# Modulation lanes gathered one block later, two multiplications moved behind the last gating, and attention heads weighed, paired and carried two steps deep

## The reference

```python
c_act = jax.nn.silu(c)
for i in range(DEPTH):
    mod = c_act @ mod_w[i] + mod_b[i]
    sh1, sc1, g1, sh2, sc2, g2, sh3, sc3, g3 = jnp.split(mod, 3 * N_SUB, axis=-1)
    h = modulate(rmsnorm(x, norm_g[i, 0]), sh1, sc1)
    x = x + FFN_RES * g1[:, None, :] * swiglu(h, ffn_w13[i, 0], ffn_w2[i, 0])
    h = modulate(rmsnorm(x, norm_g[i, 1]), sh2, sc2)
    ...
    m = mla_mixer(h, positions, mla_w_in[j], ...)
    x = x + g2[:, None, :] * m
    ...
```

## Time and profile before

| | |
|---|---|
| time, median of 3 runs | 1790.68 us (1790.57 to 1794.25) |
| the profiled execution's own time | 1786.12 us |
| its span, first to last instruction | 1784.3 us |
| mean granted clock of TensorE | 0.996 |
| TensorE busy with matmuls | 1700.4 us, 95% of the span |
| VectorE, ScalarE, GpSimd busy | 1289.4, 939.7 and 86.6 us |
| the chain that ended last | PE 62%, DVE 18%, issue 10%, ACT 8% |

### The profile page before, as it was taken

How to read it: one execution, slowest core, us unless ns; L and a number is a source line. 1 busy time by engine, 2 the same in 40 slices (tenths; PEclk the granted TensorE clock), 3 DMA queues, 4 the chain that set the end, 5 groups by cost and what they waited for, 6 DMA issues and landing times.

```text
span 1784.3 us, 32112 instructions
## 1 busy us (share of the span) xinstructions
PE 1700.4 (95%) x11300; PEld 1525.6 (85%) x11300; DVE 1289.4 (72%) x2157; ACT 939.7 (53%) x1667; POOL 86.6 (5%) x151
## 2 busy tenths in 40 slices
PE   6999999999999999999999999999999999999998
PEld 5899989888999889998778888899977788988886
DVE  6888878768888888866556666689687465556665
ACT  1444457644444444445665555545377755555553
POOL 2000011200000000000001000100000000000000
PEclk9999999999999999999999999999899999999999
DMA  9888866757888788864335666354532154446562
GB/s 349 305 299 305 279 180 201 161 212 258 297 305 263 269 301 297 301 182 143 118 95 133 208 186 190 104 179 145 159 95 78 48 186 159 149 133 200 183 185 67
DMA packets 123656, 352.76 MB, mean 198 GB/s; under 512 B 9850, under 2 KB 52874, under 8 KB 114224
## 3 DMA queue, kind: packets, MB, share of 16 engines
q1 hardware_dynamic: 108128, 262.18, 45.7%
q10 hardware_dynamic: 12432, 78.65, 13.8%
q0 software_dynamic: 3008, 10.74, 1.9%
HBM read 347.31 MB, written 4.22 MB: 197 GB/s over the span
## 4 chain that ended last, share of the span: by engine, by line
PE 62%; DVE 18%; issue 10%; ACT 8%; ACTq 1%; DMA 1%; POOL 1%; DVEq 1%; POOLq 0%
PE ps L829 39%; PE ps L1062 8%; DVE arena L358 4%; PE ps L1063 4%; DVE w_lo L195 3%; ACT w_hi L1116 2%; DVE w_lo L1127 2%; ACT w_hi L189 2%; PE ps L2992 1%; PE ps L3078 1%; DMA resid<-in_x 1%; DVE act_s L1195 1%; DVE resid L1319 1%; ACTq L332 1%; DVE arena L2685 1%
## 5 line engine op out<-in xcount | busy, mean ns | idle before, releaser
L829 PE MATMUL ps<-t_both,w_hi 128*128 128x256 f32 x3952 | 730.3, 286 | 12.8 <-DVE t_both L758 5.7
L829 PEld LDWEIGHTS ps<-t_both,w_hi 128*128 128x128 f32 x3952 | 617.7, 191 | 30.8 <-issue 15.6
L829 PE MATMUL ps<-t_both,w_lo 128*128 128x256 f32 x1976 | 560.4, 284 | 1.0 <-issue 1.0
L829 PEld LDWEIGHTS ps<-t_both,w_lo 128*128 128x128 f32 x1976 | 378.5, 192 | 0.2
L195 DVE TENSOR_TENSOR w_lo<-raw,w_hi 128x1024 fp32r<-128x1024 f32 x240 | 289.2, 1224 | 120.1 <-ACT w_hi L189 119.8
L1127 DVE TENSOR_TENSOR w_lo<-raw,w_hi 128x1024 fp32r<-128x1024 f32 x258 | 313.6, 1221 | 80.5 <-ACT w_hi L1116 80.5
L1116 ACT ACTIVATE w_hi<-raw 128x1024 fp32r<-128x1024 f32 x258 | 268.1, 1053 | 111.4 <-PE ps L829 71.6
L189 ACT ACTIVATE w_hi<-raw 128x1024 fp32r<-128x1024 f32 x240 | 248.4, 1053 | 142.5 <-PE ps L829 99.0
L1062 PE MATMUL ps<-t_both,w_hi 128*128 128x512 f32 x640 | 226.7, 398 | 0.0
L829 PE MATMUL ps<-w_hi,g_hi 128*128 128x512 f32 x440 | 174.8, 397 | 8.1 <-DVE g_lo L1198 6.0
L1063 PE MATMUL ps<-t_both,w_lo 128*128 128x256 f32 x640 | 179.7, 281 | 0.0
(11 more groups left out here) (367 smaller groups left out, 1730.2 us busy)
## 6 DMA issues: line engine op xcount, KB each, us to landing
raw<-in_stream SPq DMA_DIRECT2D x498, 512.0 KB, 4.6
arena<-in_mod_w ACTq DMA_DIRECT2D x72, 1024.0 KB, 7.3
grow<-gate_scratch POOLq DMA_DIRECT2D x6, 512.0 KB, 7.2
u_scratch<-u_keep ACTq DMA_DIRECT2D x1, 3072.0 KB, 36.9
arena<-u_scratch POOLq DMA_DIRECT2D x8, 256.0 KB, 3.5
small<-in_small POOLq DMA_DIRECT2D x1, 1368.0 KB, 11.4
resid<-in_x POOLq DMA_DIRECT2D x1, 1024.0 KB, 18.5
arena<-in_mem POOLq DMA_DIRECT2D x1, 1024.0 KB, 5.5
```

What stands on the lines that cost most here:

```text
L829: last = TE.matmul(out, lhs, rhs, start=start and i == 0, stop=stop and i == 2)
```

## The change

- In `pe_body` the gather moves from behind block 0 to behind block 1, and in `act_body` `mod_take` from ahead of the first silu to ahead of the second.
- In the closing body `dve_body` does products 4 and 5 no longer ahead of the second gating, but behind it and its split, still ahead of the residual addition.
- In the attention `values` and `mix_tile` go, with `om`. A new `weigh` multiplies the exponentials by the inverse sums in place, a step before they are turned; there are three buffers of weights in place of two, and `turn_weights` runs one step later. A new `pair_values(j)` multiplies the values of heads 2j and 2j+1, as stationary operands of 128 x 64, with the turned weights, and writes the two heads to the lower and the upper 64 partitions of ps7, already in the layout that `mix_tile` made. `prep` no longer waits for mixed tiles, and the loop has one step more.

```diff
-                        if owes is not None and j == 0:
+                        if owes is not None and j == 1:
                             mod_gather(pe, owes, turns)
...
-                    if owes is not None and t == 0:
+                    if owes is not None and t == 1:
                         mod_take(act, owes, turns)
                     act.wait_ge(used, h0 + 2 * t + 2 + RING * i)
                     E.activation(act_s[:, t, 0:L], ps[4 + t][:, 0:L], ACT.Silu).then_inc(silu_done, 1)
...
                 for t in range(2):
-                    if mod is not None and not opening:
+                    closing = t == 1 and static and i == FG - 1
+                    if mod is not None and not opening and not closing:
                         mod_products(dve, mod, range(4 * t, 4 * t + 2), turns)
                     if not (opening and t == 1):
                         lo_next(dve, i, 2 * t, static)
...
-                    if mod is not None and t == 1 and not opening and not (late_mod and static and i == FG - 1):
+                    if mod is not None and closing:
+                        mod_products(dve, mod, range(4 * t, 4 * t + 2), turns)
+                    elif mod is not None and t == 1 and not opening:
                         mod_products(dve, mod, range(4 * t + 2, 4 * t + 4), turns)
                     if t == 1 and static and i == FG - 1 and residual is not None:
                         lo_owed.append(h0 + 3 + RING * (i + 1))
...
-        om = ar(10240, QT, D)
...
         def prep(h):
 
             @block.tensor
             def _(pe):
-                pe.wait_ge(V.sem, max(roped if h < 10 else max(roped_rest.values()), max(mixed.values(), default=0)))
+                pe.wait_ge(V.sem, roped if h < 10 else max(roped_rest.values()))
                 pe.wait_ge(A.sem, max(kept_kv[h // 8], gathered.get(h - 1, 0)))
...
+        weights = (act_s[:, 0, 0:384], act_s[:, 1, 0:384], ar(10240, 384))
+        summed = {}
+
         def softmax(h):
-            sl = act_s[:, h % 2, 0:384]
+            sl = weights[h % 3]
...
+        def weigh(h):
+            sl = weights[h % 3]
+            sums, rinv = st[:, 32 + 2 * (h % 4):34 + 2 * (h % 4)], st[:, 40 + 2 * (h % 4):42 + 2 * (h % 4)]
+
+            @block.vector
+            def _(dve):
+                dve.wait_ge(A.sem, summed[h])
+                VE.reciprocal(rinv, sums).then_inc(V.sem, V.up())
+                dve.wait_ge(V.sem, V.n)
+                for q, (lo, hi) in enumerate(((0, P), (P, 3 * P))):
+                    VE.tensor_scalar(sl[:, lo:hi], sl[:, lo:hi], rinv[:, q:q + 1], None, ALU.mult).then_inc(V.sem, V.up())
+            weighed[h] = V.n
+
         def turn_weights(h):
-            sl = act_s[:, h % 2, 0:384]
+            sl = weights[h % 3]
 
             @block.tensor
             def _(pe):
-                pe.wait_ge(A.sem, max(summed[h], copied_p.get(h - 1, 0)))
+                pe.wait_ge(V.sem, weighed[h])
+                pe.wait_ge(A.sem, copied_p.get(h - 1, 0))
                 for k in range(3):
...
-        def values(h):
-            sums, rinv = st[:, 32 + 2 * (h % 4):34 + 2 * (h % 4)], st[:, 40 + 2 * (h % 4):42 + 2 * (h % 4)]
+        def pair_values(j):
+            slot = mixed_slot[j]
 
             @block.tensor
             def _(pe):
-                pe.wait_ge(A.sem, copied_p[h])
-                pe.wait_ge(V.sem, kept_out.get(h - 1, 0))
-                for q in range(QT):
-                    for i in range(q + 1):
-                        c = q * P + i * P
-                        last = TE.matmul(ps[7][:, q * 64:(q + 1) * 64], tmp[:, h % 2, c:c + P], vm[:, i, h * 64:(h + 1) * 64],
-                                         start=i == 0, stop=i == q)
+                pe.wait_ge(A.sem, copied_p[2 * j + 1])
+                if j:
+                    pe.wait_ge(V.sem, mixed[j - 1])
+                for kt, (of, n) in enumerate(((0, L), (2 * P, P))):
+                    for odd in range(2):
+                        h = 2 * j + odd
+                        last = TE.matmul(ps[7][64 * odd:64 * odd + 64, L - n:L], vm[:, kt, h * 64:(h + 1) * 64], tmp[:, odd, of:of + n],
+                                         start=kt == 0, stop=kt == 1, tile_position=(0, 64 * odd))
                 last.then_inc(T.sem, T.up())
-            at = T.n
...
-            @block.vector
-            def _(dve):
-                dve.wait_ge(A.sem, summed[h])
-                VE.reciprocal(rinv, sums).then_inc(V.sem, V.up())
-                dve.wait_ge(T.sem, at)
-                dve.wait_ge(V.sem, V.n)
-                for q in range(QT):
-                    VE.tensor_scalar(om[:, q, h * 64:(h + 1) * 64], ps[7][:, q * 64:(q + 1) * 64], rinv[:, q:q + 1], None,
-                                       ALU.mult).then_inc(V.sem, V.up())
-            kept_out[h] = V.n
-
-        def mix_tile(j):
-            slot = mixed_slot[j]
-
-            @block.tensor
-            def _(pe):
-                pe.wait_ge(V.sem, max(kept_out.values()))
-                pe.wait_ge(A.sem, max(gathered.values()))
-                for q in range(QT):
-                    last = TE.transpose(ps[4][:, q * P:(q + 1) * P], om[:, q, j * P:(j + 1) * P], ident)
-                last.then_inc(T.sem, T.up())
-            at, done = T.n, blocks["pe"]
+            valued[j] = T.n
+            done = blocks["pe"]
 
             @block.scalar
             def _(act):
-                act.wait_ge(T.sem, at)
+                act.wait_ge(T.sem, valued[j])
                 act.wait_ge(used, done)
-                E.activation(t_hi[:, slot, :], ps[4][:, 0:L], ACT.Copy).then_inc(A.sem, A.up())
+                E.activation(t_hi[:, slot, :], ps[7][:, 0:L], ACT.Copy).then_inc(A.sem, A.up())
             hi_at = A.n
 
             @block.vector
             def _(dve):
                 dve.wait_ge(A.sem, hi_at)
-                VE.tensor_tensor(t_lo[:, slot, :], ps[4][:, 0:L], t_hi[:, slot, :].bitcast(F32), ALU.subtract).then_inc(V.sem, V.up())
+                VE.tensor_tensor(t_lo[:, slot, :], ps[7][:, 0:L], t_hi[:, slot, :].bitcast(F32), ALU.subtract).then_inc(V.sem, V.up())
             mixed[j] = V.n
             kt_ready[slot] = (V.n, hi_at)
...
-        for step in range(HEADS + 3):
+        for step in range(HEADS + 4):
             if step < HEADS:
                 prep(step)
             if step < 2:
                 kv_unit(1, 1, step, step == 1)()
             elif step < 6:
                 q_unit((step - 2) // 2, (step - 2) % 2, step == 5)
-            elif step < 18:
-                out_unit((step - 6) // 2, step % 2)
+            else:
+                out_unit((step - 6) // 2, step % 2, parts=(0,) if step == HEADS + 3 else (0, 1))
             if step == 8:
                 gate_row((mod_at(1, 5), 1.0))
-            if step >= 5 and step % 2 == 1:
-                mix_tile((step - 5) // 2)
             if 0 <= step - 1 < HEADS:
                 scores(step - 1)
-            if 0 <= step - 2 < HEADS:
-                turn_weights(step - 2)
+            if step >= 5 and step % 2 == 1:
+                pair_values((step - 5) // 2)
+            if 0 <= step - 3 < HEADS:
+                turn_weights(step - 3)
             if 0 <= step - 1 < HEADS:
                 softmax(step - 1)
-            if 0 <= step - 3:
-                values(step - 3)
+            if 0 <= step - 2 < HEADS:
+                weigh(step - 2)
             if step in (1, 2, 5, 6, 7):
                 next_split()
             elif step >= 8 and step % 2 == 0:
                 next_split(lo_later=step == 18)
-        out_unit(6, 0)
-        mix_tile(7)
-        out_unit(6, 1)
+        out_unit(6, 1, parts=(1,))
         out_unit(7, 0)
         out_unit(7, 1)
```

More of the change, by code:

```diff
@@ L2347, in build @@
         mixed_slot = (10, 11, 6, 7, 0, 1, 2, 3)
-        prepped, gathered, scored, raised, turned_p, copied_p, summed, kept_out, mixed = {}, {}, {}, {}, {}, {}, {}, {}, {}
-        mixed_hi = {}
+        prepped, gathered, scored, raised, turned_p, copied_p, weighed, valued, mixed = {}, {}, {}, {}, {}, {}, {}, {}, {}
         def prep(h):
```

## The result

The changed kernel took 1781.3 us (median of five executions, 1778.31 to 1784.13) against 1790.68 for the kernel before: a ratio of 0.9945, 95% interval 0.9934 to 0.9956, or 9 to 10 us less where 5.5 were forecast. In two later comparisons it was 0.9969 (0.9955 to 0.9982) and 0.9955 (0.994 to 0.9969). Over all executions, 16 of the changed kernel and 71 of the kernel before, the means are 1782.3 and 1790.2: 7.9 us. A seventeenth of the changed kernel, 2020.96 us at a mean granted clock of 0.773, is left out.

A forecast was written before the change was run, and what follows sets the result against it. TensorE, busy for 95% of the span, was taken as the bound. Gather 0.6, closing body 1.0 and attention 3.9 make 5.5 us less than 1786.12, so 1780.6, and 4.6 more gives a median of 1785.2; range 1781.8 to 1790.2.

The forecast's parts named there:

- The gather: TensorE's gather one block later, body 1 of calls 0 to 2: 0.6 us less, from call 0; bounds nothing and 1.6.
- `mod_place` on POOL: It follows the moved `mod_take`, and only the next body's gather waits for it: 0 us.
- The closing body: Two multiplications later in two calls: TensorE's wait falls from 1.30 to about 0.55, 1.0 us less; bounds 0.3 and 1.5.
- Attention: Paired values at 0.86 us a pair replace single values and mixed tiles: 3.9 us less in all, work and waits.
- Pairs of steps: In attention, a steady pair of steps falls from 7.80 to 6.9 us.
- the new wait for the low half: In attention, the next output unit needs the pair's low half: 0.3 us is left uncovered, taken as 0.4.
- the longer tail: At attention's end one more step stands and the last two output tiles wait for low halves: 1.5 us given back.
- rival A: In attention, the halves overlap little in this shape, a pair costs 1.3 to 1.6 us: about 1788 us; chance 0.18.
- D: In attention, every pass of a pair waits for its own weights, 2.5 us a pair: 1796.6 us; chance 0.07.
- The sum: Whole kernel: 0.6 + 1.0 + 3.9 = 5.5 us less than the profiled execution's 1786.12, so 1780.6.
- the same difference gives 1785.2: Whole kernel: the median 1790.68 lies 4.6 us above the profiled execution; this difference, kept, turns 1780.6 into 1785.2.
- Rival B: At the gather, the moved wait lets the clock fall in one or more calls: sum 3 us, 1787.7; chance 0.10.

The follow-up runs named there:

- the filled version: Changed kernel plus 16 unread products of 256 columns ending the opening body of calls 0, 1 and 2: 1780.67 us against 1782.66 for the whole change beside it.
- the two orders: Changed kernel as it is, and with a pair's four products reordered, both of the even head, then both of the odd: 1780.6 us for the reordered one, a single execution.

## Why the prediction was right and wrong

- *The gather* (0.6 forecast, bounds 0 and 1.6). The wait moved to the second gated tile of body 1 with its length, as the text said. Of the 0.6 in call 0 the traces show 0.24. That the wait is slack is shown by the filled version.
- *`mod_place` on POOL, 0.* Wrong. It named the next gather as the only one that waits for it, and overlooked the gate row's store and load queued behind it on POOL. Alone that costs 0.8 in call 0's closing. Together with the other part it shortens the closing waits to 0.55, but the row then comes too late for the residual in 9 of 27 closings. Neither the forecast nor any rival had either, and the times show no gain from it.
- *The closing body* (1.0). The profiled executions show 1.3, and the wait came out as forecast. Against the average of three profiles of the old closings it is about 2.7, with the late weights and the half speed behind them; the runs of the part gave 1.4 alone and 0.7 with the gather.
- *Attention* (3.9). The trace shows 4.2, from 0.80 a pair instead of 0.86. Pairs of steps, the new wait for the low half and the longer tail are as laid out, only the tail's last waits differ. The price rested on the right picture, that passes on the two halves overlap. The trace shows them starting 0.01 apart. So rival A's condition does not hold, and D's uncovered loads are refuted by the 0.80. The Trainium skill, "TensorEngine Tiling (Array Packing)", Key Properties, says that different tiles can load and multiply in parallel. The trace agrees: 0.80 and 0.81 in the two orders, for twice the columns that one half does in 0.80.
- *The sum* (5.5) is 5.3 in the trace, in part by luck: the gather's 0.6 did not come, and the other two parts gave 0.3 more each. **The step that failed is the last one**, "the same difference gives 1785.2": it carried the 4.6 us between the profiled execution and the median over unchanged, as though what lies between two executions had nothing to do with the change. That difference is in part late loads and half speed, and some of it sat in just those waits that the change shortens. I had read one profile, which shows neither at attention's tail or in the closings, and priced each wait at its length there. The counts put 2.7 us on that: 1.3 at attention's tail (half speed in 4 of 5 profiles before, in none of 9 after) and 1.4 in the closings, which the times bear out less well. All executions give 7.9, which lies at the edge of the first comparison's interval and inside the other two, so what the first one shows beyond it (9.4 by the medians) most likely goes with the executions that were timed.
- Rival B's mechanism is there, but it was there before: the moved wait brings half speed about as often as the old one (13 of 21 against 10 of 15). Half speed became rarer in the closings, where the wait fell to 0.55 (0.63 to 1.54 in four of 20), and at attention's tail, where it only fell from 1.53 to 1.37. Length alone does not decide: of the waits of 1.54 to 1.65 in three closings, none was followed by half speed.

What stays open: why half speed follows a given wait in one execution and not in the next, and why attention's tail is spared at 1.37. The 1.4 us of the closings rest on three profiles. That the gate row's store holds the weights up rests on the slow stretch that comes at its end in all 28 closings and moved with it; the store was not taken out alone.

## What to carry to other kernels

A wait of TensorE costs more than its length in one profile where a load can lengthen it or half speed can follow it: price it from several profiles. A wait that only moves gains nothing; put work into it, even useless work, and see whether time and clock change: that tells slack from loss. When a step moves, follow every queue it stands on down to the transfers behind it, and to who waits for those.

## What the runs showed of the hardware

- TensorE fell to half speed behind waits of 1.5 to 2.8 us at the same places of the same kernel in some executions and not in others; behind a wait of 1.56 to 1.60 near 281 us it did so in none of 14 profiles. 16 products put in front of the wait, which cut it to 0.5 to 0.9, left no half speed in six bodies.
- Float32 products on the two halves of 64 columns ran side by side in either order of issue: 0.80 and 0.81 us for eight passes of 1536 columns in all, and 0.80 for four passes of 768 columns on one half.
- While the gate's 1024 numbers were stored, 4 KB in 9.6 to 12.2 us from issue to landing, the DMA engines moved 32 to 108 GB/s in the last 6 us in all 28 closings of calls 0 and 1, and 364 to 416 beside the 512 KB load behind it (from 1 us after its issue). A 1 MB load issued 1.7 us behind the store took 12.4 to 14.0 us (ten of ten), one issued 4.2 us ahead of it 6.3 to 9.3 (15 of 18).
